# Where the weight splits of a gated MLP stand on ScalarE's and VectorE's queues

## The reference

```
# first block, layer 0:   out = (silu(h @ wg) * (h @ wu)) @ wd
# second block, both layers:
u = causal_dwconv(h @ w_up + b_up, dw_w, dw_b)      # depthwise, 3 taps over positions
out = (silu(u[..., :2816]) * u[..., 2816:]) @ w_down
```

## Time and profile before

| | |
|---|---|
| runs | 2852.48, 2855.63, 2859.88 us; median 2855.63 |
| profiled execution | 2855.63 us, its span 2853.8 us |
| busy in the span | PE (TensorE) 2681.0 us, DVE (VectorE) 2200.3 us, ACT (ScalarE) 1511.9 us, POOL (GpSimd) 47.5 us |
| mean granted TensorE clock | 0.962 |
| MLP of the first block | 217.6 to 425.1 us |
| MLP of the second block, layer 0 | 2051.5 to 2238.6 us |
| MLP of the second block, layer 1 | 2659.2 to 2846.2 us |

### The profile page before, as it was taken

One profiled execution on the slowest core, in us unless ns is written; L12 is line 12 of the kernel. 1 busy time (PEld: TensorE's weight loads), 2 busy tenths in 40 slices (PEclk: granted clock), 3 DMA queues, 4 the chain that ended last, 5 costly groups with the idle time before them and its releaser, 6 DMA issues.

```text
span 2853.8 us, 37596 instructions
## 1 busy us (share of the span) xinstructions
PE 2681.0 (94%) x15600; PEld 2354.1 (82%) x15600; DVE 2200.3 (77%) x2517; ACT 1511.9 (53%) x1541; POOL 47.5 (2%) x77
## 2 busy tenths in 40 slices
PE   6879998979999999999999799899899999998998
PEld 5769987868888888888888699878799898787898
DVE  6877767678889888888888789835587798554777
ACT  3323335447777777777776464334454554244554
POOL 2000000000000000000000000000000000000000
PEclk9879999989999999999999899999999999999999
DMA  8748863369999999999999552354355533363453
GB/s 305 252 141 324 322 228 126 104 199 367 354 347 359 349 357 350 356 351 346 360 350 356 184 176 91 114 181 162 104 189 181 168 113 119 118 200 110 158 196 112
DMA packets 367904, 661.98 MB, mean 232 GB/s; under 512 B 26601, under 2 KB 191087, under 8 KB 363631
## 3 DMA queue, kind: packets, MB, share of 16 engines
q1 hardware_dynamic: 351104, 657.04, 65.6%
q10 hardware_dynamic: 16623, 2.47, 0.5%
HBM read 657.63 MB, written 1.84 MB: 231 GB/s over the span
## 4 chain that ended last, share of the span: by engine, by line
PE 82%; DVE 10%; ACT 3%; issue 2%; DMA 2%; POOL 1%; ACTq 0%; DVEq 0%; POOLq 0%; SPq 0%
PE PS L420 23%; PE PS L422 23%; PE PS L421 23%; PE PS L498 3%; PE PS L2311 2%; PE PS L2325 2%; DVE LO L415 2%; ACT HI L406 2%; DMA RAW<-in_w_ada_dram 1%; DVE AR L651 1%; PE PS L1716 1%; PE PS L2190 1%; PE PS L1752 1%; DVE RAW L651 1%; PE PS L2181 1%
## 5 line engine op out<-in xcount | busy, mean ns | idle before, releaser
L415 DVE TENSOR_TENSOR LO<-RAW,HI 128x2048 fp32r<-128x2048 f32 x410 | 930.5, 2274 | 301.6 <-ACT HI L406 301.4
L406 ACT ACTIVATE HI<-RAW 128x2048 fp32r<-128x2048 f32 x410 | 779.4, 1903 | 365.4 <-PE PS L422 320.8
L420 PE MATMUL PS<-X1H,HI 128*128 128x256 f32 (+1 forms) x2128 | 613.4, 288 | 6.0 <-DVE LO L415 4.5
L421 PE MATMUL PS<-X1L,HI 128*128 128x256 f32 (+1 forms) x2128 | 607.0, 285 | 0.0
L422 PE MATMUL PS<-X1H,LO 128*128 128x256 f32 (+1 forms) x2128 | 606.5, 285 | 0.0
L420 PE MATMUL PS<-HI,X1H 128*128 128x512 f32 x1056 | 430.9, 408 | 3.1 <-DVE LO L415 3.1
L420 PEld LDWEIGHTS PS<-X1H,HI 128*128 128x128 f32 (+1 forms) x2128 | 411.3, 193 | 10.7 <-DVE LO L415 5.0
L421 PEld LDWEIGHTS PS<-X1L,HI 128*128 128x128 f32 (+1 forms) x2128 | 411.1, 193 | 2.7 <-issue 0.5
L422 PE MATMUL PS<-HI,X1L 128*128 128x512 f32 x1056 | 413.3, 391 | 0.0
L421 PE MATMUL PS<-LO,X1H 128*128 128x512 f32 x1056 | 412.6, 391 | 0.0
L422 PEld LDWEIGHTS PS<-X1H,LO 128*128 128x128 f32 (+1 forms) x2128 | 410.8, 193 | 1.0
(11 more groups left out here) (387 smaller groups left out, 2932.2 us busy)
## 6 DMA issues: line engine op xcount, KB each, us to landing
RAW<-in_w_in_dram SPq DMA_DIRECT2D x66, 1024.0 KB, 5.1
RAW<-in_expert_w_gate_dram SPq DMA_DIRECT2D x66, 1024.0 KB, 5.2
RAW<-in_expert_w_up_dram SPq DMA_DIRECT2D x64, 1024.0 KB, 5.3
RAW<-in_expert_w_down_dram SPq DMA_DIRECT2D x62, 1024.0 KB, 5.4
RAW<-in_ffn_w_up_dram SPq DMA_DIRECT2D x55, 1024.0 KB, 5.3
AR<-in_expert_w_down_dram SPq DMA_DIRECT2D x50, 1024.0 KB, 5.4
AR<-in_expert_w_up_dram SPq DMA_DIRECT2D x48, 1024.0 KB, 5.5
AR<-in_expert_w_gate_dram SPq DMA_DIRECT2D x46, 1024.0 KB, 5.2
```

The costliest lines, as they stand in the source:

```text
L406: a.activation(HI[:, n % NH, 0:size(i)], raw_at(i), ACT.Copy).then_inc(*hi.up(i))
L415: v.tensor_tensor(LO[:, m % NH, 0:n], raw_at(i), HI[:, m % NH, 0:n].bitcast(F32), ALU.subtract).then_inc(*lo.up(i))
L420: t.matmul(o, lh, rh, start=first, stop=False)
L421: t.matmul(o, lh, rl, start=False, stop=False)
```

## The change

In the second block each pair now makes two splits (one in the last pair) before its first bias copy, none between the copies but one in the last pair, and one after the hidden tile from pair 1 on. In the first block the last two pairs are treated as the others are: one split after the hidden tile in each, so that the next stage's units are split one or two places earlier on VectorE, ahead of the diagonal tiles, and the last sum of the modulation goes into `done`. TensorE's explicit wait for that sum is taken out. The number of splits and their order in the stream stay the same.

```diff
@@ pe_ffn1
         def before_end():
-            t.wait_ge(*dve_ada("mod", 5))
             pe_late_params(t, 0)
@@ act_ffn1
-            if 0 < p < N_PAIRS - 2:
+            if p > 0:
                 split_hi(a)
-        split_hi(a)
-        split_hi(a)
         act_residual(a, 0, 1)
@@ dve_ffn1
         def done(n, p):
-            if n in (10, 19):
+            if n in (10, 19, 30):
                 dve_ada_sum(v, 2 + n // 9, 2 * ((p + 1) % 2))
-            split_lo(v)
+            if n < 32:
+                split_lo(v)
...
-        for p in range(1, N_PAIRS - 1):
+        for p in range(1, N_PAIRS):
             done(3 * p - 1, p)
             done(3 * p, p)
             hidden(p)
-            if p < N_PAIRS - 2:
-                done(3 * p + 1, p)
+            done(3 * p + 1, p)
             if p in (1, 2):
                 dve_gains(v, 0, 0, p - 1)
-        split_lo(v)
-        split_lo(v)
-        hidden(N_PAIRS - 1)
-        dve_ada_sum(v, 5, 2)
         dve_diag(v, (0, 1), MOD[:, 0, 40:48])
         dve_combine(v, 0, 1)
-        split_lo(v)
-        split_lo(v)
         dve_residual(v, 0, 1, "ffnd", lambda: None)
@@ act_layer2
         for p in range(N_PAIRS):
+            split_hi(a)
+            if p < N_PAIRS - 1:
+                split_hi(a)
             for q, nm in ((0, "g"), (1, "u")):
...
                 z.then_inc(*act_ffn.up(key, "pad", p, q))
-                split_hi(a)
                 if q == 0:
+                    if p == N_PAIRS - 1:
+                        split_hi(a)
                     a.wait_ge(*dve_ffn(key, "conv", p, 0))
...
             act_hidden(a, key, p, CV[:, p % 2, 2:4, :].rearrange("p c n -> p (c n)"))
-            if 0 < p < N_PAIRS - 2:
+            if p > 0:
                 split_hi(a)
-        split_hi(a)
-        split_hi(a)
@@ dve_layer2
         for p in range(N_PAIRS):
+            split_lo(v)
+            if p < N_PAIRS - 1:
+                split_lo(v)
             for q in range(2):
...
-                if q == 0:
+                if q == 0 and p == N_PAIRS - 1:
                     split_lo(v)
...
             dve_hidden(v, key, p, hv.rearrange("p c n -> p (c n)"))
-            split_lo(v)
-            if 0 < p < N_PAIRS - 2:
+            if p > 0:
                 split_lo(v)
-        split_lo(v)
-        split_lo(v)
         add_x(key + "d", "ffnx")
```

## The result

The changed kernel takes 2889.66 us (median of 4 runs, 2888.4 to 2892.48) against 2856.3 (4 runs) before: ratio 1.0118, 95% interval 1.0101 to 1.0136, so 33.4 us slower; 2885 had been forecast. The profiled execution took 2892.93 us around a span of 2891.1.

What follows compares the result with a forecast made beforehand. TensorE, busy 94% of the span and never waiting in the second block's steady pairs, was taken as the bound. 4.94 + 10.96 + 10.99 + 2.4 = 29.3 us on 2855.63 gave 2885, range 2874 to 2896.

Steps and rivals of the forecast that it cites:

- No gain to be had in the steady part: Second block's FFN, steady pairs: TensorE is busy 17.00 of 17.00 us, so moving splits can give nothing back.
- The chain starts a unit later, d0 and d1 wait: Second block, first two pairs: chain to hidden tile starts 5.7 us later; first down unit 2.27 us late, second 1.38 more.
- The ring of 17.14 us: Second block, steady pairs: VectorE and ScalarE's closed loop paces TensorE, 0.16 us slower than its 16.98, eight times: 1.28 us.
- The tail: Second block, last two pairs: TensorE waits before the last down unit, 6.64 us in layer 0, about 6.1 in layer 1.
- What comes back in layer 0: End of layer 0's MLP: the LO no longer holds the residual additions past the last matmul, minus 0.61 us.
- The first block: End of its MLP: diagonals stand behind a LO, row sums start 5.23 us late; net 4.94 us slower.
- TensorE's clock: Half-rate restart after three stalls, ahead of the row sums and each layer's last down unit: 0.8 us each, 2.4 in all.
- My cap of 1.5 us a stall: After each of the three stalls: a half-clock stretch of 3.4 us loses at most 1.5 us.
- this upper end: Top of the clock term, 4.5 us: all three stalls pay for the slow restart, going by the Trainium skill alone.

Runs made afterwards that it cites:

- early only in pairs 9 and 10: Kernel before the change, with the second block's splits moved early only in the last two pairs, first block as before; ratio 1.0051.
- diagonals-first kernel: Changed kernel, with the first block's diagonals and combination made ahead of the LO of the next stage's second unit; 2885.9 us.
- keeping TensorE busy: Changed kernel, with 46 extra unused matmuls ahead of the wait before the last down unit in the second block; 2886.74 us against 2889.66.
- first-block kernel: Kernel before the change, with only the first block's part of the change; 2867.01 us, ratio 1.0034.

## Why the prediction was right

- **No gain to be had in the steady part.** Right; the stages where only pairs run never became shorter.
- **The chain starts a unit later, d0 and d1 wait.** d0 came 2.2 us late (forecast 2.27), d1 another 0.9 (forecast 1.38).
- **The ring of 17.14 us.** Too long. VectorE's LO of d1 begins a row of three LOs at 2104.62 and the next pair's begins at 2121.53 in the changed kernel: 16.91. The link "SiLU to the next bias copy 0.74" was the mistake: in the changed kernel it is 0.53 or 0.54 (2248.45 to 2248.98 above), since in the earlier trace rows the bias copy had waited for TensorE's u1. With 0.54 the ring is 16.94, just under TensorE's 16.98, and the same 0.20, taken twice, is most of d1's error of 0.44. Yet the steps after d1 cost 0.6 to 0.7 us together (forecast 1.28), mostly at d3, d5 and d7. Each of these starts just behind its LO, 0.1 us late, and 0.1 more is lost in its first matmuls. Why it is every second pair was not worked out.
- **The tail.** The profile's waits are 6.30 and 5.65 us; they count from the modelled end of the matmul before, which overlaps the next. Counted by starts, as the forecast counts, d10 is delayed by 6.63 and 5.95 us more than d9; the forecast was 6.64 and 6.06. Such closeness is in part luck: LO 2217.38 is 0.12 later than its own links give (2215.31 + 1.95), the link of 0.20 too much is in this chain too, and from the hidden remainder to d10 it took 0.15 us and not 0.04. In all d10 came 10.60 and 10.01 us late in the stage, forecast 11.57 and 10.99. The kernel that is early only in pairs 9 and 10 shows that the wait is made there.
- **What comes back in layer 0.** As forecast: d10's last matmul is later by 13.56 us, the next norm's first transpose by 12.94, so 0.62 come back (forecast 0.61). The next stage's first product is later by 12.60; the rest is the clock at the transposes.
- **The first block.** The wait is 5.08 us (5.0 forecast), ended by the diagonals, and the row sums start 5.24 us late (forecast 5.23); the diagonals-first kernel shows that the LO is its cause, and its time shows that taking out TensorE's wait on the sum gave nothing.
- **TensorE's clock: the term that was mis-sized.** Forecast 2.4 us for three stalls. Measured 2.2 in the first block (the row sums take 3.44 us instead of 1.70, and d10's sixth matmul starts 0.5 later after its first), 2.4 in layer 0 and 1.5 in layer 1 (both shown by keeping TensorE busy): 6.1 us. I had let half of the slow stretch fall into the idle time; in fact the clock was at the lower level for the first 3.1 us of work or more in all three, and in layer 0 for 5.7. My cap of 1.5 us a stall was wrong as well, since it took the slow stretch to be as short as the 3.4 us one of the earlier trace rows. The Trainium skill ("TensorE: Matmul & The Clock Gate", on the HAM clock gate) would have had all three pay; the traces agree with it (0.50, 0.50 and 0.52 after the idles). The forecast should have taken this upper end, and even that, 4.5 us, was too low.

The two errors partly cancel: about 1.6 us too much in the chains, 3.8 too little in the clock, so 31.5 us by stages against 29.3. That the point of 2885 us lies as near as 4.7 us to the measured 2889.66 owes something to that. The mechanism, with the place and the engine that ends each wait, stands without it.

## What to carry to other kernels

On an in-order queue, place a prefetch so that what it waits for is already done when the queue reaches it: a split that must wait for the consumer's last use drags everything behind it, and a steady loop hides most of that once its first two iterations have paid (3.4 us, then 0.6 to 0.7), while its last iterations, where less of the consumer's work is left as cover, cannot. Work out the chain of the last two iterations link by link, and take each link from a row where nothing else was being waited for. Price an idle of TensorE of 5 us or more with its slow restart: here 1.5 to 2.4 us on top of the wait. Keep small GpSimd steps of a norm clear of long two-input work on VectorE.

## What the runs showed of the hardware

GpSimd's addition of two columns took 1.42 us instead of 0.20 while VectorE subtracted two SBUF tiles, and ended 0.05 to 0.06 us after VectorE's instruction, five times of five; with that instruction moved away it took 0.19. The Trainium skill ("SBUF — State Buffer", the section on who interferes with whom) says that a VectorE instruction with two SBUF inputs and a GpSimd instruction that reads SBUF exclude each other; the traces agree.

TensorE's clock fell to 0.50 after each idle of 5 us and more that the change made, and not after those of 2.07 and 0.79 us: from 2088.9 to 2124.9 us, which takes in the work behind both, it was 1.00:

```profile
2088.90:2124.90 36.00, 35.16 (x244) 32.92 (x245) 27.87 (x35) 17.82 (x20) 0.00 (x0) 1.00 0.42 147
```

The drift of runs goes with the clock as well. In the 13 runs of the kernel before that were timed beside the first-block kernel, those of 2859.8 us and more have a mean granted clock of 0.959 or 0.960, those of 2856.8 us and less 0.961 or 0.962. The profiles show one such place: the first-block kernel was 5.3 us longer between 590 and 1640 us, and the same 121 matmuls took 40.2 us at a mean clock of 0.67 (600.5 to 640.7 us) and 35.0 us at 0.82 in the kernel before (595 to 630 us), with VectorE equally busy, 22.46 us. Why the clock differs there, in work that the edit does not touch, is open; no run was made for it.
